# The cumulated log gate of the fox attention: as matmuls into the scores, or as a masked bias that is broadcast through DRAM

## The reference

```python
log_f = jax.nn.log_sigmoid(fg + b_f)            # (B, 8, S)
cum = jnp.cumsum(log_f, axis=-1)
s = jnp.einsum('bhqd,bhkd->bhqk', qi, k) * scale
s = s + ci[..., :, None] - cum[..., None, :]     # ci: cum of the query's own position
mask = key_pos[None, :] <= qpos[:, None]
p = jax.nn.softmax(jnp.where(mask, s, -jnp.inf), axis=-1)
```

## Time and profile before

| | |
|---|---|
| median of 3 runs | 779.28 us (779.02 to 779.87) |
| the profiled execution | 780.31 us |
| its span in the trace | 778.3 us |
| busy: TensorE, DVE, ACT, POOL | 98%, 60%, 51%, 8% of the span |
| the chain that ended last | 96% TensorE |
| DMA | 158.71 MB, mean 204 GB/s |

### The profile page before, as it was taken

One profiled execution on the slowest core, in us unless ns is written; L12 is line 12 of the kernel. 1 busy time (PEld: TensorE's weight loads), 2 busy tenths in 40 slices (PEclk: granted clock), 3 DMA queues, 4 the chain that ended last, 5 costly groups with the idle time before them and its releaser, 6 DMA issues.

```text
span 778.3 us, 10523 instructions
## 1 busy us (share of the span) xinstructions
PE 766.1 (98%) x4083; PEld 621.4 (80%) x4083; DVE 469.3 (60%) x616; ACT 393.4 (51%) x562; POOL 64.9 (8%) x84
## 2 busy tenths in 40 slices
PE   8999999999999999999999999999999999999996
PEld 6668766878888898888788877777898888888885
DVE  4468676587766554636774435447568776545355
ACT  2447877454344343535534466666455545334363
POOL 2115121010000000002440000000010000000011
PEclk9999999999999999999999999999999999999999
DMA  9999478828766467567487635316475655563601
GB/s 292 331 354 344 163 276 331 322 72 301 240 231 201 124 222 254 164 193 254 161 298 237 204 109 193 127 59 187 139 228 165 195 184 182 197 196 128 216 27 55
DMA packets 91024, 158.71 MB, mean 204 GB/s; under 512 B 3319, under 2 KB 34259, under 8 KB 89952
## 3 DMA queue, kind: packets, MB, share of 16 engines
q1 hardware_dynamic: 88336, 151.04, 58.7%
q0 software_dynamic: 2352, 6.91, 2.7%
q10 hardware_dynamic: 288, 0.10, 0.1%
HBM read 156.95 MB, written 1.08 MB: 203 GB/s over the span
## 4 chain that ended last, share of the span: by engine, by line
PE 96%; DVE 1%; ACT 1%; issue 1%; POOLq 0%; POOL 0%; ACTq 0%; DVEq 0%
PE PS L1057 24%; PE PS L1059 23%; PE PS L1058 23%; PE PS L1069 6%; PE PS L1070 3%; PE PS L1308 2%; PE PS L1268 2%; PE PS L1120 2%; PE PS L1022 1%; PE PS L1337 1%; PE PS L1363 1%; PE PS L1214 1%; PE PS L1079 1%; PE PS L1078 1%; PE PS L1080 1%; PE PS L1293 1%
## 5 line engine op out<-in xcount | busy, mean ns | idle before, releaser
L1705 DVE TENSOR_TENSOR wlo<-raw,whi 128x2048 fp32r<-128x2048 f32 (+3 forms) x124 | 278.6, 2250 | 147.6 <-ACT whi L1454 131.5
L1454 ACT ACTIVATE whi<-raw 128x2048 fp32r<-128x2048 f32 (+3 forms) x124 | 226.1, 1823 | 159.4 <-PE PS L1059 156.9
L1057 PE MATMUL PS<-whi,hT 128*128 128x512 f32 (+1 forms) x568 | 223.0, 393 | 0.9 <-issue 0.5
L1059 PE MATMUL PS<-whi,hT 128*128 128x512 f32 (+1 forms) x568 | 216.7, 382 | 0.0
L1058 PE MATMUL PS<-wlo,hT 128*128 128x512 f32 (+1 forms) x568 | 216.4, 381 | 0.0
L1057 PEld LDWEIGHTS PS<-whi,hT 128*128 128x128 f32 x568 | 106.9, 188 | 25.0 <-issue 5.3
L1059 PEld LDWEIGHTS PS<-whi,hT 128*128 128x128 f32 x568 | 106.8, 188 | 21.1
L1058 PEld LDWEIGHTS PS<-wlo,hT 128*128 128x128 f32 x568 | 107.1, 188 | 18.2
L1057 PE MATMUL PS<-whi,hidT 128*128 128x512 f32 x216 | 84.4, 391 | 0.0
L1059 PE MATMUL PS<-whi,hidT 128*128 128x512 f32 x216 | 84.1, 389 | 0.0
L1058 PE MATMUL PS<-wlo,hidT 128*128 128x512 f32 x216 | 84.1, 389 | 0.0
(11 more groups left out here) (274 smaller groups left out, 823.4 us busy)
## 6 DMA issues: line engine op xcount, KB each, us to landing
raw<-in_w_in SPq DMA_DIRECT2D x34, 1024.0 KB, 5.3
raw<-in_w_ff SPq DMA_DIRECT2D x32, 1024.0 KB, 5.3
raw<-in_w_ada SPq DMA_DIRECT2D x16, 1024.0 KB, 6.2
raw<-in_w_gate SPq DMA_DIRECT2D x10, 1024.0 KB, 5.6
raw<-in_w_up SPq DMA_DIRECT2D x10, 1024.0 KB, 5.2
raw<-in_w_down SPq DMA_DIRECT2D x10, 1024.0 KB, 5.0
raw<-in_w_ada SPq DMA_DIRECT2D x16, 512.0 KB, 7.5
raw<-in_w_out SPq DMA_DIRECT2D x8, 1024.0 KB, 5.7
```

The source lines that it names most:

```text
L1057: pe.matmul(o, ah, wh, start=(k == 0), stop=False)
L1059: return pe.matmul(o, al, wh, start=False, stop=end)
L1454: act.activation(split_view(whi, i)[:, c], slab_view(raw, slot, i)[:, c], ACT.Copy).then_inc(hi_made if i else part_whi, 1)
L1705: dve.tensor_tensor(split_view(wlo, i)[:, c], slab_view(raw, slot, i)[:, c], whole(split_view(whi, i))[:, c], ALU.subtract).then_inc(lo_ma ...
```

## The change

The gate no longer enters by matmuls. The sign of the log gate is turned in DVE's steps, so that the cumulated sum is already minus the cumulated log gate. ACT writes it to DRAM, `f_dram`, 8 rows of 384: the 256 keys, and the first 128 once more. From there it is read back into `fbias` with the row of each head repeated on all 128 partitions: pair 0 by ACT (`fcast`), pairs 1 to 3 by POOL, behind pair 0's. POOL then writes the mask's value over the keys that lie after the query, by an affine select on the last 256 of the 384 columns (the diagonal block of either query block). DVE's reduction takes `fbias` in place of the mask. The identity copy `identr`, `ncum` and the load of the mask go away; the load of the distance biases moves from behind `unit:1` to behind POOL's three broadcasts. `fbias` lies over the gate's own buffers.

The constants table loses the mask's columns, and STAGE and the number of setup loads are changed to suit; the rest in its core:

```diff
@@ plan(), the common order
-    order += [("fgate", 0), ("unit", 0), ("unit", 1), ("logf", 0)] + early
+    order += [("fgate", 0), ("unit", 0), ("unit", 1), ("logf", 0), ("fcast", 0)] + [("fbias", u) for u in range(FOX_P)] + early
@@ ACT_ORDER
-split:8 split:9 EV:fox0 EV:fox1 EV:fox2 split:10 fgate:0 split:11 logf:0 heads:0 split:12 heads:1 scores:0
+split:8 split:9 EV:fox0 EV:fox1 EV:fox2 fgate:0 split:10 logf:0 split:11 fcast:0 heads:0 split:12 heads:1 scores:0
@@ DVE_ORDER
-split:8 split:9 EV:fox0 fgate:0 EV:fox1 split:10 unit:0 unit:1 logf:0 split:11 scores:0 scores:1 probs:0
+split:8 split:9 EV:fox0 fgate:0 EV:fox1 unit:0 logf:0 split:10 unit:1 split:11 scores:0 scores:1 probs:0
@@ build(), tensors
+        f_dram = nc.dram_tensor("f_dram", [FOX, 3 * P], F32, kind="Internal")
-        ncum = sb("ncum", [P, 2, S], F32R, g)
+        gg.close()
+        fbias = sb("fbias", [P, FOX, 3 * P], F32, g)
-        identr = sb("identr", [P, P], F32R)
-        mask = con[:, C_MASK:C_MASK + 2 * P]
+        def f_rows(u):
+
+            return bass.AP(tensor=f_dram, offset=2 * u * 3 * P, ap=[[0, P], [3 * P, 2], [1, 3 * P]])
@@ TensorE, fgate and scores
-                    reader[6] = [(cum_made, 1)]
+                    reader[6] = [(fg_abs, 1)]
-                    if u == 0:
-                        pe.wait_ge(zeroed, 1)
-                        pe.wait_ge(ncum_lo, 1)
-                                             kT[r, slot, 0:c1 - c0], start=True, stop=not picks)
-                            if t == 1 and not picks:
+                                             kT[r, slot, 0:c1 - c0], start=True, stop=True)
+                            if t == 1:
                                 last.then_inc(score_ps, 1)
-                        for part in range(2 * picks):
-                            for n, r in enumerate(rows):
-
-                                pick = identr[r, n * HD + 2 * u + n:n * HD + 2 * u + n + 1].to_broadcast([HD, P])
-                                last = pe.matmul(PS[:, 5 + n, c0:c1], pick, ncum[r, part, 0:c1 - c0], start=False,
-                                                 stop=part == 1)
@@ ACT, logf and fcast
                     act.wait_ge(cum_made, 1)
-                    act.wait_ge(zeroed, 1)
-                    act.activation(ncum[0:GATE, 0, :], fgt[:, 3, :], ACT.Copy, scale=-1.0).then_inc(ncum_hi, 1)
+                    act.dma_start(f_dram.ap()[:, 0:S], fgt[0:FOX, 3, :]).then_inc(f_out, 16)
+                    act.dma_start(f_dram.ap()[:, S:S + P], fgt[0:FOX, 3, 0:P]).then_inc(f_out, 16)
+
+                elif kind == "fcast":
+
+                    act.wait_ge(f_out, 32)
+                    act.dma_start(fbias[:, 0:2, :], f_rows(0)).then_inc(fbias_in[0], 16)
@@ DVE, setup, fgate, logf and scores
-                    dve.tensor_copy(identr[:, :], ident)
-                    dve.tensor_scalar(fgt[:, 0, :], PS[0:GATE, 6, 0:S], bf[:, :], None, ALU.add).then_inc(fg_abs, 1)
+                    dve.tensor_scalar(fgt[:, 0, :], PS[0:GATE, 6, 0:S], bf[:, :], -1.0, ALU.add, ALU.mult
+                                      ).then_inc(fg_abs, 1)
-                                                  op0=ALU.min, op1=ALU.subtract))
+                                                  op0=ALU.max, op1=ALU.add))
-                    dve.scalar_tensor_tensor(out=ncum[0:GATE, 1, :], in0=fgt[:, 3, :], scalar=-1.0,
-                                             in1=whole(ncum[0:GATE, 0, :]), op0=ALU.mult, op1=ALU.subtract
-                                             ).then_inc(ncum_lo, 1)
-                            if a == 0:
-                                dve.wait_ge(setup_in, 16 * NSETUP)
-                            bias = [mask[:, P:2 * P], mask]
+                            dve.wait_ge(fbias_made, u + 1)
+                            bias = [fbias[:, a, S:S + P], fbias[:, a, 0:S]]
@@ POOL, setup, unit 1 and fbias
-            pool.memset(ncum[:, :, :].bitcast(F32), 0.0).then_inc(zeroed, 1)
-                    pool.dma_start(con[:, C_MASK:C_ALIBI], A["constants"][:, C_MASK:C_ALIBI]).then_inc(setup_in, 16)
                     if i == 1:
                         pool.wait_ge(part_lo, KC)
+
+                elif kind == "fbias":
+
+                    pool.wait_ge(fbias_in[i], 16)
+                    if i == 0:
+                        pool.wait_ge(f_out, 32)
+                        for u in range(1, FOX_P):
+                            pool.dma_start(fbias[:, 2 * u:2 * u + 2, :], f_rows(u)).then_inc(fbias_in[u], 16)
                         pool.dma_start(alibi[:, :, :], A["constants"][:, C_ALIBI:C_HOT].rearrange("p (h k) -> p h k", h=DIFF)
                                        ).then_inc(alibi_in, 16)
+                    b = fbias[:, 2 * i:2 * i + 2, P:3 * P].rearrange("p h (b k) -> p h b k", b=2)
+                    pool.affine_select(out=b, in_=b, compare_op=ALU.is_ge, fill=MASKED, base=0,
+                                       pattern=[[0, 2], [0, 2], [-1, P]], channel_multiplier=1).then_inc(fbias_made, 1)
```

More of the change, by code:

```diff
@@ L53 @@
 FF = len(FF_AT)
-STAGE = 19820
-C_ID, C_MASK, C_ALIBI, C_HOT = 0, 128, 384, 1408
+STAGE = 20204
+C_ID, C_ALIBI, C_HOT = 0, 128, 1152
 C_ALL = C_HOT + SKEW
@@ L486, in build @@
         AB = sb("AB", [P, 4, KC], F32, g)
-        wfgs = sb("wfgs", [P, 2, KC, GATE], F32R, g)
-        bf = sb("bf", [GATE, 1], F32, g)
-        fgt = sb("fgt", [GATE, 4, S], F32, g)
-        ones = sb("ones", [GATE, S], F32, g)
         valT = sb("valT", [P, S], F32, g)
-        ncum = sb("ncum", [P, 2, S], F32R, g)
         hss = sb("hss", [P, 4, TB * 8], F32, g)
@@ L496, in build @@
         drs = sb("drs", [P, TB * DIFF], F32, g)
+        gg = ExitStack()
+        wfgs = sb("wfgs", [P, 2, KC, GATE], F32R, gg)
+        bf = sb("bf", [GATE, 1], F32, gg)
+        fgt = sb("fgt", [GATE, 4, S], F32, gg)
+        ones = sb("ones", [GATE, S], F32, gg)
+        gg.close()
+        fbias = sb("fbias", [P, FOX, 3 * P], F32, g)
         od = tok1[:, 1]
@@ L668, in build @@
         cum_made = sem("cum_made")
-        ncum_hi = sem("ncum_hi")
-        ncum_lo = sem("ncum_lo")
+        f_out = sem("f_out")
+        fbias_in = [sem(f"fbias_in{u}") for u in range(FOX_P)]
+        fbias_made = sem("fbias_made")
         tok_in = sem("tok_in")
@@ L919, in squares_of @@
             return (None, xnb, xnb, None, None, fin)[n][:, t, h * W:(h + 1) * W]
-        NSETUP = 6
+        NSETUP = 5
         QB = ((0, P), (P, 3 * P))
@@ L1305, in _ @@
                     for t, (c0, c1) in enumerate(QB):
-                        picks = kind_of(u) == "fox"
                         for n, r in enumerate(rows):
                             last = pe.matmul(PS[:, 5 + n, c0:c1], qT[r, slot, t * P:(t + 1) * P],
-                                             kT[r, slot, 0:c1 - c0], start=True, stop=not picks)
-                            if t == 1 and not picks:
+                                             kT[r, slot, 0:c1 - c0], start=True, stop=True)
+                            if t == 1:
                                 last.then_inc(score_ps, 1)
-                        for part in range(2 * picks):
-                            for n, r in enumerate(rows):
-                                pick = identr[r, n * HD + 2 * u + n:n * HD + 2 * u + n + 1].to_broadcast([HD, P])
-                                last = pe.matmul(PS[:, 5 + n, c0:c1], pick, ncum[r, part, 0:c1 - c0], start=False,
-                                                 stop=part == 1)
-                                if (t, part) == (1, 1):
-                                    last.then_inc(score_ps, 1)
                     for n in range(2):
@@ L1451, in _ @@
                     if i < KC:
-                        act.wait_ge(zeroed, 3)
+                        act.wait_ge(zeroed, 2)
                         act.activation(gate_homes(0, i), gate_columns(slot), ACT.Copy).then_inc(wfg_hi, 1)
@@ L1769, in _ @@
                 elif kind == "setup":
-                    dve.wait_ge(cond_in, 32)
-                    dve.tensor_copy(identr[:, :], ident)
                     dve.memset(ones[:, :], 1.0).then_inc(ones_made, 1)
@@ L1915, in _ @@
                     then(dve.scalar_tensor_tensor(out=fgt[:, 2, :], in0=fgt[:, 0, :], scalar=0.0, in1=fgt[:, 1, :],
-                                                  op0=ALU.min, op1=ALU.subtract))
+                                                  op0=ALU.max, op1=ALU.add))
                     dve.tensor_tensor_scan(fgt[:, 3, :], ones[:, :], fgt[:, 2, :], 0.0, ALU.mult, ALU.add
                                            ).then_inc(cum_made, 1)
-                    dve.wait_ge(ncum_hi, 1)
-                    dve.wait_ge(cum_made, 1)
-                    dve.scalar_tensor_tensor(out=ncum[0:GATE, 1, :], in0=fgt[:, 3, :], scalar=-1.0,
-                                             in1=whole(ncum[0:GATE, 0, :]), op0=ALU.mult, op1=ALU.subtract
-                                             ).then_inc(ncum_lo, 1)
```

(5 more changed lines are left out.)

## The result

The changed kernel takes 785.65 us (median of 6, 783.62 to 786.0) against 779.33 us for the kernel before: the ratio is 1.0074, 95% interval 1.0064 to 1.0084. It is slower, by 6.3 us by the medians and 5.8 by the ratio, where 1.85 had been forecast; the time lies above the stated range of 778.0 to 784.6. The six executions differ: four took 785.55 to 786.0 us with a mean granted TensorE clock of 0.993 or 0.994, two took 783.62 and 784.23 with 0.995. The profiled one is of the first kind: it took 785.75 us, of which 783.9 are its span.

What follows compares the result with a forecast made beforehand. TensorE, busy for 98% of the span, was taken as the bound. A wait of +3.65 us less 1.8 us of picks gave +1.85, so 781.1 us for the median, with an 8-in-10 range of 778.0 to 784.6.

Steps and rivals of the forecast that it cites:

- the place and the kind: TensorE idle once, before the second fox pair's scores, ended by DVE's reductions, these by POOL's select; wait 3.65 us.
- The gate's part on DVE and ACT: Cumulated gate: with ACT's and DVE's new order the sum is ready at 70.6 instead of 74.34.
- the picks' gain: TensorE: pick matmuls removed from the fox scores save 0.45 us a pair, 1.8 us over four pairs.
- the write: Gate to DRAM, issued by ACT: landing at 75.5, 3.6 us after the second issue; ends 73.3 and 77.4.
- the loaded rows: Profile rows of small DRAM writes under load, 4.7 and 5.8 us against 1.7, set against the skill's rule.
- I take 3.0: Pair 0's broadcast of 384 KB, issued at 75.5: 3.0 us, landing at 78.5; ends 2.5 and 5.6.
- the weights' load end: DMA load around the write: without the distance biases in it, it ends near 75.2.
- POOL's issues: Three broadcasts and the distance biases issued ahead of pair 0's select: 3.05 us, until 81.6; ends 2.1 and 0.
- the select: POOL's select for pair 0: 0.95 us, half of 1.87 for 128x1024, ending at 82.6.
- a wait of some 4 us: Before the second fox scores: past this wait TensorE's clock may fall, adding 3.0 us.
- slow ends: Rival at pair 0's bias: late write and broadcast, clearly slower; 16% together with a fallen clock.
- The other branch of that rival: Write landed at 77.4, broadcast 5.6 us: bias at 87.1, wait 8, net +6.3, 785.6; within the 16%.

Runs made afterwards that it cites:

- held transfers: Changed kernel, but SP holds its next 1 MB weights transfer until pair 0's broadcast is in; 783.81 us, ratio 1.0054.
- idle-work experiment: Changed kernel with ten idle matmul pairs on TensorE ahead of its wait for pair 0's reductions; 782.75 us, ratio 1.0045.
- idle-work runs: Ten idle pairs added to the changed kernel, 782.75 us; five added to its version with POOL's three broadcasts issued beside pair 0's, 781.13 us against 783.28.
- early-bias kernel: Changed kernel, but ACT reads pair 0's bias early from a constant table, without waiting for the gate (wrong bias); 778.02 us, ratio 0.9986.
- hybrid: Kernel before with the changed order and sign: pair 0 keeps picks and mask, pairs 1 to 3 take the broadcast; 779.35 us, 0.9994; repeated, 779.21 us.
- hybrids: Pair 0 by picks, pairs 1 to 3 by broadcast: 779.35 and 779.21 us; with pair 0's division before pair 1's reduction on DVE, 779.45 us.

## Why the prediction was wrong

- Right: the place and the kind. TensorE waits once, before the second fox pair's scores, for DVE, DVE for POOL's select, POOL for the broadcast. The gate's part on DVE and ACT came as worked out, 70.3 for 70.6 (70.1 when carried to this execution's earlier start).
- Right in kind: the picks' gain, 1.8 us in the sum, 1.4 (0.9 to 2.3) measured alone.
- Right in sum: the write. Carried to the same start of the program it was forecast to land at 75.0 and landed at 74.9, issued 0.4 us earlier and 0.35 longer under way. By the rule of the Trainium skill ("DMA: Bandwidth & Descriptors", "Anatomy of one DMA"), about 2.0 us, it would, by that estimate, have been there at 73. The Trainium skill fits that figure to DMAs issued by POOL, and these were issued by ACT. The measurement decides: the loaded rows were the better guide.
- The step that failed, first: "I take 3.0" for pair 0's broadcast. It took 5.0, and POOL went on 5.5 after the issue. I had read it from 512 KB of weights, against a loaded broadcast of 5.6 us in the same group. I had the weights' load end at 75.2, from the old order, and overlooked that the change moves it: SP issues 1 MB at 72.97 (before, 71.04) and again at 76.3, into the same window. The held transfers show 1.5 us of sharing in it.
- Too large: POOL's issues, 3.05 in the sum, took 2.23, and the select 0.66 for 0.95. So the wait came to 3.65 + 2.5 - 1.1 = 5.05; measured 5.0.
- The step that failed, second and larger: the clock. I put the loss of 3 us behind "a wait of some 4 us", because the one row of an idle TensorE at the end of the span showed it down after that long, and gave the case a small chance. A wait of 5.0 costs 2.9 us more by the idle-work experiment (2.3 by the ratios, 3.3 by the traces); in the traces the clock also fell at waits of 3.4, 2.6 and 2.4 us and not at one of 2.3. With the wait of 3.65 that I forecast, the clock's part would have belonged in the sum: 779.3 + 1.85 + 2.9 = 784.1, an estimate. The size of that part was right, 3.0 against 2.9.
- The rule of the Trainium skill beside it ("TensorE: Matmul & The Clock Gate", Part 1), that the slow clock is the default and activity lifts it, agrees with the idle-work runs: with idle matmuls in the wait the granted clock stayed at 1.00 in both traces, and 2.9 and 2.15 us came off.

The rival "slow ends", 785.0 with a wait of 4.5 us and the fallen clock, is what happened; slow ends and a fallen clock together had been given 16%. The other branch of that rival names 785.6, almost the time measured, but from a wait of 8 us at full clock, and no such wait was there.

## What to carry over

When a value goes through DRAM instead of an engine that is the bound, price the trip by the loaded rows, put the transfers that the streaming queue will issue in that very window into it, and look at what stands on the issuing engine between the landing and the use. Look also at whether the change moves those transfers: an engine's new order moves the splits, and with them the next loads. A wait of TensorE costs its length and may cost the clock behind it, here some 2 to 3.7 us, already at waits near 2.5 us; idle matmuls in front of an unavoidable wait bring that part back, real work in front of it brings both. And a gain of half a microsecond at each of four places is gone when the first of them has 0.6 us of slack.

## What was not expected of the hardware

- The granted clock at waits in the middle of dense work: down at 5.0, 3.44, 2.62 and 2.39 us, still 1.00 at 2.31 us. With waits so close together and different outcomes, these traces don't show that length alone decides, nor what else does.
- The select (128x512) took 0.63 to 0.66 us in most places, but 1.89 and 2.40 us for pair 3's, in the early-bias kernel and the hybrid, both times beside DVE's split of a slab. No other of the bias's selects traced here overlaps a split. Both long ones end 0.50 us after the split does (85.73 after 85.23, 85.89 after 85.39), as if POOL had stood still beside it. A scalar operation of POOL (L2139) shows the same: 1.24 us, ending 0.06 after DVE's scaling beside it, where it took 0.20 alone (L2147 in the kernel before). No run was made to separate the two engines, so the cause is argued from these ends.
- The same broadcast of 384 KB, issued at the same place beside two others and the weights, ended between 79.5 and 82.0 us in three executions of the hybrids (79.50, 80.76, 82.02). Pair 0's, in the four kernels with three others issued beside it, ended at 79.76, 80.81, 80.88 and 81.58. One trace of such a kernel says little about a slack of 2 us.
- A write of 12 KB in two DMAs to DRAM took 4.2 us on loaded engines, from the second issue to the broadcast's, and 4.4 with the weights behind it held back; the other kernels with ACT's broadcast show 3.1 to 4.3.
